# Hymba-style decoder layer on one core: first row blocks by column halves, early weight slots, other units for passes and copies

## What is computed

```python
def reference(x, w_in, conv_w, mix_norm_g, w_out, ln1_g, ln1_b, w_gate_up, w_down, ln2_g, ln2_b):
    proj = x @ w_in
    q, k, v, qi, ki, wi, gate_b, gate_c, h = _split_cols(proj, IN_SPLIT_SIZES)
    q, k, qi, ki = rotary(q), rotary(k), rotary(qi), rotary(ki)
    attn_out = _dsa_attention(q, k, v, qi, ki, wi)      # score = sum_h w_h relu(qi_h . ki); the 256 best keys of a query
    conv_out = gate_b * causal_conv3(gate_c * h)
    mixed = concat(rms_norm(attn_out), rms_norm(conv_out)) * mix_norm_g
    x = layer_norm(ALPHA * x + mixed @ w_out)
    gate, up = split(x @ w_gate_up)
    return layer_norm(ALPHA * x + (silu(gate) * up) @ w_down)
```

## Time and profile before

| | before |
|---|---|
| median of 3 runs | 1249.62 us (1249.06 to 1250.3) |
| profiled execution | 1250.92 us, of which the span 1249.1 us |
| PE busy | 1221.5 us, 98% of the span |
| DVE busy | 951.7 us, 76% |
| POOL busy | 673.2 us, 54% |
| ACT busy | 524.4 us, 42% |
| chain that ended last | PE 89%, DVE 5%, ACT 2%, POOL 2%, DMA 1% |

### The profile page before, as it was taken

The page is one execution under the profiler, slowest core; times in us unless marked ns, Lnnn a source line. Parts: engine busy times, 40 slices in busy tenths (PEclk is TensorE's granted clock), DMA queues, the critical chain, the costliest instruction groups (busy, mean ns, idle before and its releaser), DMA issues.

```text
span 1249.1 us, 17037 instructions
## 1 busy us (share of the span) xinstructions
PE 1221.5 (98%) x6037; PEld 1031.1 (83%) x6037; DVE 951.7 (76%) x1535; ACT 524.4 (42%) x917; POOL 673.2 (54%) x552
## 2 busy tenths in 40 slices
PE   8999999999999999999999999999999999999997
PEld 7978788888878899788788888888888888888885
DVE  4668999999988889437878677776776766565897
ACT  4466322321358889503543332333323333654351
POOL 2240667896978541108978767566666630020744
PEclk9999999999999999999999999999999999999999
DMA  5232122220011111424145544544544448966664
GB/s 203 73 89 47 39 51 59 68 66 20 18 24 45 35 38 65 161 83 145 52 135 185 169 160 136 194 140 147 190 142 158 160 169 296 350 194 191 198 190 164
DMA packets 121405, 157.66 MB, mean 126 GB/s; under 512 B 7253, under 2 KB 81257, under 8 KB 119913
## 3 DMA queue, kind: packets, MB, share of 16 engines
q1 hardware_dynamic: 121320, 156.57, 38.9%
HBM read 109.09 MB, written 40.11 MB: 119 GB/s over the span
## 4 chain that ended last, share of the span: by engine, by line
PE 89%; DVE 5%; ACT 2%; issue 2%; POOL 2%; DMA 1%; DVEq 0%; ACTq 0%; POOLq 0%
PE banks L707 26%; PE banks L709 26%; PE banks L708 26%; PE banks L923 2%; PE banks L974 2%; PE banks L869 1%; DVE scores L1954 1%; PE banks L943 1%; PE banks L942 1%; PE banks L891 1%; PE banks L890 1%; DVE pt L2044 1%; PE banks L1053 0%; PE banks L723 0%; POOL w_lo L1540 0%
## 5 line engine op out<-in xcount | busy, mean ns | idle before, releaser
L1970 DVE TENSOR_SCALAR_CACHE_REDUCE mask<-scores,small 128x384 bf16<-128x384 f32 (+1 forms) x186 | 163.7, 943 | 1.1
L2301 DVE TENSOR_TENSOR step_lo<-step_raw,step_hi 128x1024 fp32r<-128x1024 f32 x77 | 110.1, 1450 | 57.4 <-ACT step_hi L1487 56.9
L1733 POOL TENSOR_TENSOR ring_lo<-sum,ring_hi 128x512 fp32r<-128x512 f32 x88 | 122.5, 1394 | 58.2 <-ACT ring_hi L1423 58.2
L707 PE MATMUL banks<-act_hi,ring_hi 128*128 128x512 f32 x352 | 137.2, 390 | 0.0
L709 PE MATMUL banks<-act_hi,ring_lo 128*128 128x512 f32 x352 | 137.0, 389 | 0.0
L708 PE MATMUL banks<-act_lo,ring_hi 128*128 128x512 f32 x352 | 137.0, 389 | 0.0
L1733 POOL TENSOR_TENSOR ring_lo<-gu_raw,ring_hi 128x512 fp32r<-128x512 f32 x66 | 96.1, 1458 | 65.2 <-ACT ring_hi L1423 65.2
L1487 ACT ACTIVATE step_hi<-step_raw 128x1024 fp32r<-128x1024 f32 x77 | 81.7, 1061 | 111.1 <-DMA step_raw<-in_w_down 55.8
L1423 ACT ACTIVATE ring_hi<-sum 128x512 fp32r<-128x512 f32 x88 | 55.0, 630 | 166.4 <-POOL sum L1744 64.6
L707 PE MATMUL banks<-step_hi 128*128 128x512 f32 x308 | 119.9, 389 | 0.0
L708 PE MATMUL banks<-step_lo,step_hi 128*128 128x512 f32 x308 | 119.8, 389 | 0.0
(11 more groups left out here) (266 smaller groups left out, 3137.8 us busy)
## 6 DMA issues: line engine op xcount, KB each, us to landing
gu_raw<-in_w_gate_up SPq DMA_DIRECT2D x44, 512.0 KB, 5.1
step_raw<-h_store SPq DMA_DIRECT2D x77, 256.0 KB, 3.0
wd_raw<-in_w_down SPq DMA_DIRECT2D x11, 1024.0 KB, 4.9
h_store<-hid SPq DMA_DIRECT2D x11, 1024.0 KB, 3.9
step_raw<-wd_store SPq DMA_DIRECT2D x44, 256.0 KB, 3.9
wd_store<-wd_raw SPq DMA_DIRECT2D x11, 768.0 KB, 3.4
h_store<-h_sum SPq DMA_DIRECT2D x11, 768.0 KB, 5.4
step_raw<-in_w_down SPq DMA_DIRECT2D x33, 256.0 KB, 3.3
```

The source lines that it names most:

```text
L707: pe.matmul(dst, a[0], b[0], start=first, stop=False)
L1733: pool.tensor_tensor(ring_lo[:, slot], src, ring_hi[:, slot].bitcast(F32), ALU.subtract).then_inc(ring_low, 1)
L1970: c = dve.tensor_scalar(mask[:, part(b)], scores[:, part(b)], threshold(j), 0.0, ALU.is_ge, ALU.add, accum_out=count[:, j:j + 1])
L2301: dve.tensor_tensor(step_lo[n][:], step_raw[n][:], step_hi[n][:].bitcast(F32), ALU.subtract).then_inc(step_low, 1)
```

## The change

1. Blocks 0 and 1 of x are loaded as column halves (256 KB each), with their own semaphores, in the order: half 0 of block 0, slot 0, half 0 of block 1, slots 1 to 3, the two second halves, slots 4 and 5, block 2, slots 6 and 7, block 3, constants, blocks 4 to 7. Blocks 4 and 5 share a semaphore, as do 6 and 7.
2. PE turns the two first halves, and the second halves in front of k 2 and k 3 of the first pair, blocks 2 and 3 in front of k 6 and k 7 (before: in front of k 4 and k 6). ACT's list goes along.
3. The tiles of blocks 0 and 1 of group 0 take the columns 256 to 327 only (key and head weights), `columns_of`.
4. The slots 4 to 7 have raw slots of their own, `w_raw_early`.
5. Units 0 to 11 take four passes each, later ones two (four at heads 1 of the blocks from 5 on); the copies to gate_c come at the units 12 and 13.
6. At the block before the last, both `query_low` and `key_low` of the last block come behind head 0.
7. ACT splits the slots 26 and 27 at the units 44 and 46, and POOL lowers them before the convolution.
8. Semaphores: the stores of x1 of the last two blocks share one, and the loads of ln2_g and ln2_b use `ln_loaded`.

```diff
-        ENTRY_WEIGHTS = {1: (0, 1, 2, 3), 2: (4, 5), 3: (6, 7)}
+        X_TURNS = [(0, 0), (1, 0), (0, 1), (1, 1)] + [(b, half) for b in range(2, NB) for half in range(2)]
...
+        PAIR_UNITS = 6 * KT // 4
+        def raw_slot(s):
+            return w_raw_early[:, s - 4, :] if 4 <= s < KT else w_raw[:, s % 4, :]
+        def columns_of(m):
+            g, _, b = tiles[m]
+            n = groups[g][2]
+            return (AW // 2 if g == 0 and b not in SEL else 0), n
         def passes_of(i):
-            if i < TWO_BANKS - 2:
-                return 4 if i < 6 else 3
-            return 4 if i >= TWO_BANKS and i % HEADS == 1 else 2
+            if i < PAIR_UNITS:
+                return 4
+            return 4 if i > TWO_BANKS + HEADS and i % HEADS == 1 else 2
...
-                if s >= 4:
-                    sp.wait_ge(w_low, s - 3)
+                if s >= KT:
+                    sp.wait_ge(w_low, s - 3 if s >= KT + 4 else s - KT + 1)
...
+            load_x(0, 0)
+            load_w(0)
+            load_x(1, 0)
+            for s in (1, 2, 3):
+                load_w(s)
+            load_x(0, 1)
+            load_x(1, 1)
+            load_w(4)
+            load_w(5)
+            load_x(2)
+            load_w(6)
+            load_w(7)
+            load_x(3)
...
+                        if g == 0 and pair[1] == outs[1]:
+                            if k in (2, 3):
+                                turn_half(k - 2, 1)
+                            elif k in (6, 7):
+                                turn_x(k - 4)
+                        elif g == 0 and k in (4, 6) and pair[1] != outs[-1]:
                             turn_x(tiles[pair[1]][2] + k // 2 - 1)
...
-            x_high(0)
-            splits(2)
-            x_high(1)
+            splits(1)
+            half_high(0, 0)
+            half_high(1, 0)
+            splits(4)
+            half_high(0, 1)
+            half_high(1, 1)
             splits(6)
-            x_high(2)
+            half_high(2, 0)
+            splits(7)
+            half_high(2, 1)
             splits(KT)
             x_high(3)
...
+                    if i in (len(unit_idx) - 4, len(unit_idx) - 2):
+                        splits(3 * KT + 3 + (i - len(unit_idx) + 4) // 2)
...
-            for s in range(3 * KT, 3 * KT + 2):
+            for s in range(3 * KT, 3 * KT + 4):
                 split_low(s)
...
+                    elif b == NB - 2 and h == 0:
+                        query_low(NB - 1, 0)
+                        query_low(NB - 1, 1)
+                        key_low(NB - 1)
```

More of the change, by code:

```diff
@@ L277, in build @@
         w_loaded = [sem(f"w_loaded{s}") for s in range(4)]
+        w_early = [sem(f"w_early{n}") for n in range(2)]
         w_high, w_low, w_used = sem("w_high"), sem("w_low"), sem("w_used")
@@ L311, in build @@
         x1_turned, x1_hi, x1_lo = sem("x1_turned"), sem("x1_hi"), sem("x1_lo")
-        x1_stored = [sem(f"x1_stored{b}") for b in range(NB)]
+        x1_stored = [sem(f"x1_stored{b}") for b in range(NB - 1)]
         pairs_summed, last_summed = sem("pairs_summed"), sem("last_summed")
@@ L540, in load_constants, with load_x @@
                 sp.dma_start(par_raw[12:20, :], mix_norm_g[0].rearrange("(c p) -> c p", p=P)).then_inc(const_loaded, 16)
[L542 to L547, removed]
+            def load_x(b, half=None):
+                cols_ = slice(0, DM) if half is None else slice(512 * half, 512 * half + 512)
+                sp.dma_start(xs[:, b, cols_], x_rows[b][:, cols_]
+                             ).then_inc(x_loaded[b if b < 4 else b // 2 * 2, half], 16)
+            load_x(0, 0)
[11 more added lines that the diff above has]
+            load_x(3)
+            load_constants()
+            for b in range(4, NB):
+                load_x(b)
             def spread_idx(b):
@@ L712, in _, with turn_half @@
             pe.wait_ge(ident_made, 1)
-            def turn_x(b):
[L716 to L724, removed]
+            def turn_half(b, half):
+                n = X_TURNS.index((b, half))
+                if b < 2:
+                    pe.wait_ge(x_loaded[b, half], 16)
+                elif b < 4:
+                    pe.wait_ge(x_loaded[b, None], 16)
+                else:
+                    pe.wait_ge(x_loaded[b // 2 * 2, None], 32)
+                if n >= 4:
+                    pe.wait_ge(xt_lo, n - 3)
+                for j in range(4):
+                    k = 4 * half + j
+                    t = pe.transpose(X_BANK[n % 4][:, j * P:(j + 1) * P], xs[:, b, k * P:(k + 1) * P], ident[:])
+                t.then_inc(xt_ready, 1)
+            def turn_x(b):
+                turn_half(b, 0)
+                turn_half(b, 1)
             def turn_parameters():
@@ L803, in project @@
                     for k in range(KT):
[L804 to L808, removed]
+                        if g == 0 and k in (0, KT // 2):
+                            pe.wait_ge(xt_lo, X_TURNS.index((tiles[pair[1]][2], 2 * k // KT)) + 1)
+                        if g == 0 and pair[1] == outs[1]:
[4 more added lines that the diff above has]
+                        elif g == 0 and k in (4, 6) and pair[1] != outs[-1]:
                             turn_x(tiles[pair[1]][2] + k // 2 - 1)
@@ L847, in _ @@
                     for n in range(3)]
-            assert sum(passes_of(i) for i in range(TWO_BANKS - 2)) == len(fill) // 3
+            assert sum(passes_of(i) for i in range(PAIR_UNITS)) == len(fill) // 3
             filled = [0]
@@ L1141, in _, with half_high @@
         def _(act):
-            def x_high(b):
-                for half in range(2):
-                    n = 2 * b + half
-                    act.wait_ge(xt_ready, n + 1)
-                    act.activation(act_hi[:, 4 * half:4 * half + 4, b * P:(b + 1) * P],
-                                   X_BANK[n % 4].rearrange("p (k s) -> p k s", k=4), ACT.Copy).then_inc(xt_hi, 1)
+            def half_high(b, half):
+                n = X_TURNS.index((b, half))
+                act.wait_ge(xt_ready, n + 1)
+                act.activation(act_hi[:, 4 * half:4 * half + 4, b * P:(b + 1) * P],
+                               X_BANK[n % 4].rearrange("p (k s) -> p k s", k=4), ACT.Copy).then_inc(xt_hi, 1)
+            def x_high(b):
+                half_high(b, 0)
+                half_high(b, 1)
             def copy_parameters():
@@ L2397, in apply_gain @@
                 if q == 0:
[L2398 removed]
+                    dve.wait_ge(ln_loaded, 64)
                 if q >= 2 and first == 0:
```

73 lines of the change are left out of this document (41 added, 32 removed).

## The result

The changed kernel takes 1256.82 us (median of 4 runs, 1256.36 to 1257.47); the kernel before took 1249.34 us beside it. The ratio is 1.0049 with a 95% interval of 1.0035 to 1.0064: slower by 0.5%, well beyond the 0.2% that can be told from no change. The forecast was 1251.1 with a range up to 1255.5. So the likeliest case was wrong, the time is outside the range, and what happened is the rival "the clock comes late" in its last form ("up to 1257"). The two profiled executions differ by less, 1256.8 against 1250.92, because the one of the kernel before lies 1.6 us above its median.

What follows compares the result with a forecast made beforehand. TensorE, busy 98% of the span, was taken as the bound. Opening +1.5 and middle 0.0 summed to +1.5 on the median of 1249.62, giving 1251.1 us, range 1247.4 to 1255.5.

Steps and rivals of the forecast that it cites:

- the clock comes late: Rival, opening: PE's clock rises later because less work precedes it; slower, 1252.5 to 1257 us, chance 0.32.
- last form: Opening: the level rises only once the wide matmuls of blocks 2 and 3 run; +6 to +8 us, up to 1257.
- the chain that the forecast was added up from: Opening: loop through PE, ACT, DVE and POOL, putting the start of blocks 2 and 3 at 20.0 us instead of 18.5.
- The sign that the prediction had named for it: Opening: narrow matmuls still 0.2 us apart behind 12 us would show the forecast wrong, by the clock.
- The page that was weighed: Opening: the skill's rule that transposes do not count as busy for the clock; the prediction said the trace disagrees.
- The loop, +1.5: Opening: ACT's new order delays splits through four engines; +1.5 us despite 2.1 us less PE work.
- Price of a narrow matmul, 0.11: Opening: a 72-column matmul taken at 0.11 us where wide ones are 0.154 apart; 48 change, 2.1 us less PE work.
- Middle: Index scores to key and query turns: PE's -1.5 us capped by DVE to 0.0; ends -1.6 and +0.6.
- Gate_c's wait: Index scores, unit 16: PE's 1.6 us wait for ACT's copies would go, with 0.5 us taken as gained.
- that for w_lo: Near 137 us: PE's wait for POOL's low weight half would go whole, -1.0 us.
- the cap: Near 346 us: PE's transposes of q wait for DVE's low halves of k, so PE gains at most 0.6 us there.
- Low clock in the attention: Rival, start of the attention: a shifted arrival lengthens or shortens the half-clock stretch, 1 to 2 us either way; chance 0.10.

Runs made afterwards that it cites:

- e5_dense: The changed kernel with 19 spare transposes in front, 12 more ahead of the wait for slot 4 and 10 ahead of slot 6; 1.0013.
- e6_whole_narrow: The changed kernel with whole blocks 0 and 1, 16 leading transposes and the earlier ACT list, narrow columns kept; 1.0028 against the kernel before.
- e9: e6_whole_narrow with 13 spare transposes ahead of the first block of x; 1.0015 against the kernel before.
- e12: e10 with 13 spare transposes ahead of the first block and DVE's order of e11_k_low; 1246.51 us, 0.9970 against the kernel before.
- e4: The kernel before with 13 spare transposes ahead of the first block of x; 0.9990.
- e2_warm: The changed kernel with 19 spare transposes in PE's idle time ahead of its first matmul; 1.0029 against the kernel before.
- e3_middle: The kernel before with items 5 to 7 of the change alone, its opening unchanged; 1.0001.
- e11_k_low: e3_middle with the first three k_low on DVE ahead of the fourth block's masks, three more before the fifth's last step; 1247.63 us, 0.9967.
- e7: The changed kernel with ACT's splits 4 and 5 ahead of the second halves' copies, 6 and 7 ahead of block 2's; 1.0035.
- e10: e6_whole_narrow with all 328 columns again for blocks 0 and 1; 0.9999 against the kernel before.
- e8: The changed kernel with ACT's order of e7, spare transposes in PE's holes and DVE's order of e11_k_low; 0.9979 against the kernel before.
- e1: The changed kernel with all 328 columns again for blocks 0 and 1, order, halves and early slots kept; 1.0034 against the kernel before.

## Why the prediction was wrong, point by point

- **The chance of the clock (the step that failed).** The mechanism was named, as a rival, and its price was nearly right: "+6 to +8, up to 1257" stands against 8.7 us lost in the opening and 1256.8. What failed is the chain that the forecast was added up from: it lets only k 0 run at the early pace (6 x 0.21) and every k behind it at 6 x 0.11. The runs showed all eight k at 0.21 and the transposes of blocks 2 and 3 at 0.20 each, and with the first wide matmuls at 0.27 that is worth 6.7 of the 8.7 us or more (e5_dense). With that failed the weighing, 0.32 for all forms of the rival against 0.42. The reason given against it was that a slow engine fills its time and so looks busy. e6_whole_narrow shows an engine without a hole for 13 us that stayed at 1.2 GHz. The argument had no row behind it: no stretch of the trace before had 72-column matmuls in a row. The sign that the prediction had named for it, narrow matmuls still 0.2 apart behind 12 us, came true.
- **The page that was weighed.** The Trainium skill ("TensorE: Matmul & The Clock Gate", Part 4: PE-mode transpose) has transposes not count as busy. I set it aside by the trace, and the runs bear that out: with nothing but transposes from 1.5 us the level was up at 4.4 to 5.2 us (e9, e12, e4); with 16 transposes alone it was up at 8.6 in before, but not by 9.1 in e6. But the conclusion that I drew from it, that the clock was safe, was about transposes, and the matmuls were the trouble. The Trainium skill ("TensorE: Matmul & The Clock Gate", Part 1: The HAM clock gate) says that the warm-up is a matter of time and not of the number of matmuls. e6 disagrees for this stream: 13.2 us of narrow matmuls and transposes without a hole did not bring it.
- **The loop, +1.5.** Right within 0.4: 1.94 in e5_dense, of which 0.6 may be its spare transposes, k 4 at 13.2 in e2_warm for 13.1. The first narrow matmul came at 7.97 and not 7.4, since PE could start on the second half-block only at 5.4, where its landing had been put at 4.85. (The 2.9 MB up to slot 7 are done near 10.3 at the prediction's own rate, not near 11; PE waited for no landing there.)
- **Price of a narrow matmul, 0.11.** Right at 2.4 GHz; 0.21 at 1.2.
- **Middle.** Gate_c's wait and that for w_lo went; PE had gained 2.4 by the turn of keys where I had taken 1.5: 1.3 in the scores (0.5 taken) and 1.1 behind them (1.0). This 0.5 was the term of the middle that was too small, and the cap hid it. DVE's first count was 0.3 later in e3_middle (132.73 for 132.43) and I took 0.6. The cap at DVE's k_hl was right in place and in size: 0.0 was forecast, e3_middle measured 1.0001.
- **Low clock in the attention.** It did move: from 6.8 us at 0.50 to none, worth 2.2 us in the trace, where I had 1 to 2.
- **Range.** It ended 1.3 us below the measured time. I let it reach "into the clock rival" instead of to its end.

## What to carry to other kernels

To cut a matmul from 328 to 72 columns can cost time: here the thinner stream did not bring TensorE's clock to the level that the wide one did. Ask what PE runs in the first 20 us before thinning it, and count such a cut at both levels. Where PE is the bound and gains in one place, look at once for the next instruction of another engine that it waits for; here one move in DVE's list let through 2.1 us (first logits of e11_k_low against e3_middle) that the middle had won and lost. Idle time of PE ahead of the first data could be filled with spare transposes at no cost here (e4_before_warm, 0.9990).

## What the runs showed of the hardware

- **72-column matmuls and the level.** In three kernels (after, e6, e7) the stream of 72-column matmuls and transposes ran at 1.2 GHz from the first, and in two (e9, e8) from 11.3 and 14.6 us, until 3.1 to 4.3 us after the first 328-column one: first wide one at 25.69, 22.62, 23.59, 20.64 and 20.61, level up at 28.8, 26.2, 27.3, 24.9 and 24.9. e2_warm, whose level had fallen at 14.2, took 5.4 us. The same matmuls do run at 2.4 GHz when the level is up (0.11 apart), and in e5_dense, where 128-column transposes filled most of the holes, it stayed up. Widths between 72 and 328 weren't tried.
- **The same start on two levels.** Behind 16 transposes from 4.5 us on, the level was up at 8.6 (before), 8.1 (e3), 7.4 (e10) and 7.2 (e11), and in e6 not at 9.1 with the first matmul. What decides it is not shown.
- **A half-clock stretch that comes and goes.** At the start of the attention, with the same instructions, the traces show 6.8 us at 0.50 (before, e1, e2, e10), 3.4 us (e3, e4, e5) or nothing (after, e6, e7, e9, e11, e12, e8). The mean granted clock listed with each execution tells the same of runs without a trace: of 30 executions of the kernel before, 12 had 0.997 to 0.999 (median 1249.2 us) and 18 had 0.994 or 0.995 (median 1252.6; 8 of them took about 1251 and 10 about 1252.7, for a reason that the clock doesn't tell). That is why its medians lie between 1249.3 and 1250.8, and part of why e11_k_low, with 0.998 or 0.999 in all 11 executions, is faster. Why its attention never met such a stretch is open: it starts 2.7 us earlier, and no run changed that alone. An earlier start is not enough by itself, for e12_wide_warm_k_low, 0.4 us earlier still, has 0.995 to 0.997 in 3 of its 6 executions.
